# Order of the attention steps' ScalarE copies, output scaling and output-product blocks in a two-block transformer kernel

## The reference

```python
s = jnp.einsum('bnqhgd,bnshd->bnhgqs', qb, kcat, preferred_element_type=jnp.float32)
...
s = jnp.where(valid[None, :, None, None], s - alibi, -jnp.inf)
...
m = jnp.maximum(jnp.max(s, axis=-1, keepdims=True), sink)
p = jnp.exp(s - m)
p = p / (jnp.sum(p, axis=-1, keepdims=True) + jnp.exp(sink - m))
o = jnp.einsum('bnhgqs,bnshd->bnqhgd', p.astype(v.dtype), vcat)
return o.reshape(B, T, N_Q_HEADS * D)
```

## Time and profile before

| | us |
|---|---|
| median of 3 runs | 2187.11 (2186.94 to 2187.57) |
| the profiled execution, own time | 2188.36 |
| its span in the profile | 2186.6 |
| PE busy in the span | 2043.5 |
| DVE busy | 1189.9 |
| ACT busy | 788.7 |
| mean granted TensorE clock, share of full speed | 0.972 |
| attention steps 0 to 35, from and to | 943.5 to 1056.75 |

### The profile page before, as it was taken

How to read it: one execution, slowest core, us unless ns; L and a number is a source line. 1 busy time by engine, 2 the same in 40 slices (tenths; PEclk the granted TensorE clock), 3 DMA queues, 4 the chain that set the end, 5 groups by cost and what they waited for, 6 DMA issues and landing times. The chain is left out here.

```text
span 2186.6 us, 34776 instructions
## 1 busy us (share of the span) xinstructions
PE 2043.5 (93%) x14184; PEld 1598.2 (73%) x14184; DVE 1189.9 (54%) x1773; ACT 788.7 (36%) x1361; POOL 143.9 (7%) x116
## 2 busy tenths in 40 slices
PE   7999999989999999978999999999988859999996
PEld 1577899867787787755788888878843538888884
DVE  5489665565444434655484565755335364565423
ACT  5776333334232212545431212234213234444311
POOL 0000222200101101000010101100000000000000
PEclk9999999989999999999999999999999879999998
DMA  5321000222332232310345354435300112323321
GB/s 178 109 87 39 2 4 4 81 89 87 97 98 94 96 97 81 105 39 21 107 154 191 133 185 144 157 116 190 98 21 0 57 59 89 104 93 99 135 87 39
DMA packets 60393, 200.33 MB, mean 92 GB/s; under 512 B 7904, under 2 KB 10848, under 8 KB 59232
## 3 DMA queue, kind: packets, MB, share of 16 engines
q1 hardware_dynamic: 59808, 193.91, 26.7%
q10 hardware_dynamic: 448, 4.46, 0.5%
HBM read 191.66 MB, written 6.42 MB: 91 GB/s over the span
## 5 line engine op out<-in xcount | busy, mean ns | idle before, releaser
L1129 DVE TENSOR_TENSOR wlo<-raw,whi 128x1024 fp32r<-128x1024 f32 x270 | 327.7, 1223 | 622.0 <-ACT whi L656 620.5
L656 ACT ACTIVATE whi<-raw 128x1024 fp32r<-128x1024 f32 x270 | 282.7, 1057 | 750.0 <-PE bank L1792 732.7
L1790 PE MATMUL bank<-inh,whi 128*128 128x512 f32 x1200 | 473.2, 394 | 26.5 <-DVEq L1725 16.1
L1791 PE MATMUL bank<-inl,whi 128*128 128x512 f32 x1200 | 469.9, 392 | 0.0
L1792 PE MATMUL bank<-inh,wlo 128*128 128x512 f32 x1200 | 469.6, 391 | 0.0
L1790 PEld LDWEIGHTS bank<-inh,whi 128*128 128x128 f32 x1200 | 227.0, 189 | 85.5 <-DVEq L1725 16.9
L1792 PEld LDWEIGHTS bank<-inh,wlo 128*128 128x128 f32 x1200 | 226.9, 189 | 47.7
L1791 PEld LDWEIGHTS bank<-inl,whi 128*128 128x128 f32 x1200 | 227.1, 189 | 47.2 <-issue 0.7
L1790 PE MATMUL bank<-hidh,whi 128*128 128x512 f32 x576 | 231.0, 401 | 5.8 <-DVE HR L1458 4.4
L1791 PE MATMUL bank<-hidl,whi 128*128 128x512 f32 x576 | 227.3, 395 | 0.0
L1792 PE MATMUL bank<-hidh,wlo 128*128 128x512 f32 x576 | 227.2, 395 | 0.0
(11 more groups left out here) (355 smaller groups left out, 2849.3 us busy)
## 6 DMA issues: line engine op xcount, KB each, us to landing
raw<-in_mlp_w SPq DMA_DIRECT2D x128, 512.0 KB, 3.6
ADW<-in_w_ada SPq DMA_DIRECT2D x32, 768.0 KB, 5.0
raw<-in_w_up SPq DMA_DIRECT2D x44, 512.0 KB, 3.5
raw<-in_w_in SPq DMA_DIRECT2D x28, 512.0 KB, 3.6
raw<-in_a_w_rkv SPq DMA_DIRECT2D x24, 512.0 KB, 3.4
raw<-in_w_down SPq DMA_DIRECT2D x22, 512.0 KB, 3.5
raw<-in_a_wo SPq DMA_DIRECT2D x8, 512.0 KB, 8.3
raw<-in_b_wq SPq DMA_DIRECT2D x8, 512.0 KB, 3.3
```

The lines of the kernel that those rows point to most:

```text
L656: act.activation(whi[u % SLOTS][:, :], raw[u % SLOTS][:, :], ACT.Copy).then_inc(w_hi, 1)
L1129: dve.tensor_tensor(lo[:, :], r[:, :], h[:, :].bitcast(F32), ALU.subtract).then_inc(w_lo, 1)
L1790: pe.matmul(o, w[:, wc], xh, start=start, stop=False)
L1791: pe.matmul(o, w[:, wc], xl_, start=False, stop=False)
```

## The change

It has four parts, all in the attention loop. ScalarE's step makes the copy PTR first, then the copy OR, then the exponentials. VectorE's scaling of pair p moves from step 2p+6 to step 2p+5, and the high and low parts of it from step 2p+7 to step 2p+6, so that its loop is one step shorter. TensorE's output-product blocks, two per step, move from steps 10, 11, 14, 15, ... to steps 9, 11, 13, 15, ... up to 35. No instruction is added or removed, and no buffer changes.

```diff
             for i in range(NT + 4):
+                if 2 <= i < NT + 2:
+                    k = i - 2
+                    act.wait_ge(pa.sem, pa.at(("tr", k)))
+                    if k >= 3:
+                        act.wait_ge(pa.sem, pa.at(("pv", k - 3)))
+                    act.activation(PTR[k % 3][:], PB[6][:], ACT.Copy).then_inc(aat.sem, aat.step(("ptr", k)))
+                if i >= 5 and i % 2 == 1:
+                    p = (i - 5) // 2
+                    act.wait_ge(pa.sem, pa.at(("bc", p)))
+                    if p >= 2:
+                        act.wait_ge(da.sem, da.at(("to", p - 2)))
+                    act.activation(OR[p % 2][:], PB[7][:, 0:256], ACT.Copy).then_inc(aat.sem, aat.step(("o", p)))
                 if i < NT:
...
-                if i >= 5 and i % 2 == 1:
...
-                if 2 <= i < NT + 2:
...
-            for i in range(NT + 6):
+            for i in range(NT + 5):
...
-                if i % 2 == 0 and i >= 6:
-                    p = (i - 6) // 2
+                if i % 2 == 1 and i >= 5:
+                    p = (i - 5) // 2
                     dve.wait_ge(aat.sem, aat.at(("o", p)))
...
-                if i % 2 == 1 and i >= 7:
-                    p = (i - 7) // 2
+                if i % 2 == 0 and i >= 6:
+                    p = (i - 6) // 2
...
-                if i >= 10 and (i - 10) % 4 < 2:
-                    kb = (i - 10) // 4
+                if i >= 9 and i % 2 == 1:
+                    kb, q = (i - 9) // 4, (i - 9) // 2 % 2
                     pe.wait_ge(w_lo, UBO + kb // 2 + 1)
                     pe.wait_ge(da.sem, da.at(("ol", 2 * kb + 1)))
-                    for m in range(2 * ((i - 10) % 4), 2 * ((i - 10) % 4) + 2):
+                    for m in range(2 * q, 2 * q + 2):
```

## The result

| | before | after |
|---|---|---|
| median, us | 2187.03 (2184.14 to 2187.57) | 2167.11 (2164.93 to 2168.63) |
| the profiled execution, own time | 2188.36 | 2164.93 |
| its span | 2186.6 | 2163.1 |
| PE busy in the span | 2043.5 | 2039.7 |
| attention, from the scores of step 0 to the rest of the output product, behind step 35 | 943.51 to 1056.75 = 113.24 | 941.02 to 1032.33 = 91.31 |

The changed kernel is faster: 0.9906 of the time before (95% interval 0.9894 to 0.9918), four runs beside four; the two medians alone give 0.9909. The medians differ by 19.9 us; 20.4 were forecast.

A forecast was written before the change was run, and what follows sets the result against it. TensorE, busy 93% of the span, bounds the kernel, with latency gaps in the attention. Start 6.8, four periods 10.3, last period 3.3 and end 0 sum to 20.4 us: 2187.11 - 20.4 = 2166.7, range 2160.5 to 2174.

The forecast's parts named there:

- The gaps are latency between engines, not load.: Attention, four steps: TensorE works 10.60 of 13.04 us, while DVE has only 6.33 and ACT 6.92 us of work.
- The wait labelled "ACT S" is a wait for TO.: Value product's listed 5.2 us wait: really for VectorE's TO, never exponentials; 1.03 us idle in one period.
- The period, 10.46: Four attention steps, 12 to 27: each period takes 10.46 us instead of 13.04, gaining 2.58, or 10.3 over four.
- PTR, exponentials, low part: hidden.: Attention steps: PTR over 1 us spare, exponentials end by S + 3.3 and due S + 5.9, low part S + 2.75 before S + 3.3.
- TO, "the thinnest cover": VectorE: TO ends near 2.7 us after an odd step's scores; the next scores' reading, due at 3.4, has 0.7 spare.
- Weight splits, under 0.1 each.: ScalarE's 1.05 us splits delay the next copy: under 0.1 us in each of three steps, off TensorE's path.
- The start, 6.8.: Steps 0 to 11: 4.7 us of idle gone, 0.5 from the first weight copy, 1.6 from the clock; sum 6.8.
- The end, 3.3 and 0.: Last period (13.79 to 10.46 us) gains 3.3; steps 32 to 35 gain 0, since TensorE has no gap there.
- The clock elsewhere.: Rival behind the attention: 9 us lost to short clock falls may halve (2162) or grow by half (2171); vanishing falls 0.08.
- One wait stays: Rival: VectorE late in even steps or PTR still holds transposes, about 1.0 us per period, 5 in all: 2171.7; chance 0.12.
- Nothing arrives: Rival: the later stage waits for weights and hands the gain back, 2187; chance 0.06 shared with both waits staying.
- Half speed in the dense stretch: Rival, steps 12 to 31: gapless small matmuls get half speed, periods 19.2 us, total 2213; chance 0.04.

The follow-up runs named there:

- extra_copy: Changed kernel with one more 128x512 copy of bank 6 on ScalarE ahead of PTR in 32 steps, into an unused tile; median 2168.83 us, ratio 0.9916.
- undo_dve: Changed kernel with VectorE's old places for TO (even steps) and the low parts (odd steps); median 2195.01 us, ratio 1.0036 to the kernel before.
- only_dve: Kernel before with VectorE's part of the change alone; median 2177.48 us, ratio 0.9960.
- or_last: Changed kernel with ScalarE's copy OR behind the exponentials, PTR still first; median 2168.24 us, ratio 0.9922 to the kernel before.
- undo_act: Changed kernel with ScalarE's old order (exponentials, OR, PTR); median 2167.75 us, ratio 0.9916 to the kernel before.
- V: VectorE's part of the change: TO in odd steps, low parts in even ones; alone on the kernel before, median 2177.48 us, ratio 0.9960.
- only_pe: Kernel before with TensorE's new places of the output-product blocks alone; median 2194.34 us, ratio 1.0034.
- only_act: Kernel before with ScalarE's new order alone; median 2181.76 us of ten runs, ratio 0.9977.
- recip_later: Changed kernel with VectorE's 3.35 us reciprocal of query scales moved from step 1 to step 2; median 2166.86 us, ratio 0.9914 to the kernel before.
- start_both: Changed kernel with VectorE's reciprocal moved to step 2 and two weight splits a step or two later; median 2165.35 us, ratio 0.9899 to the kernel before.
- sums_early: Changed kernel with TensorE's second set of query sums in step 0 instead of step 1; median 2165.13 us, ratio 0.9906 to the kernel before.
- S: ScalarE's part of the change: copies ahead of exponentials; alone on the kernel before, median 2181.76 us, ratio 0.9977.
- T: TensorE's part of the change: output-product blocks in every odd step; alone on the kernel before, median 2194.34 us, ratio 1.0034.

## Why the prediction was right

The forecast was 2166.7 within 2160.5 to 2174.0; the median is 2167.11. It was right in its cause as well, as the parts show, with terms that were off by up to a fifth. That the medians come within 0.5 of the forecast is partly luck: the attention in the trace gained 1.5 more than the sum.

- **"The gaps are latency between engines, not load."** Shown by the result: with no instruction fewer, TensorE idles 0.00 of 10.38 us where it idled 2.44 of 13.04. That ScalarE's load does not bound the changed kernel either is what extra_copy adds: 15.3 us more of its work cost 2.3. VectorE's load was not raised in any run.
- **The wait labelled "ACT S" is a wait for TO.** Shown: with TO back in the even step (undo_dve) the value product waits 1.11 behind it, with it in the odd step (only_dve, and after) there is no such wait, whatever ScalarE's order is.
- **The period, 10.46.** It came out at 10.38 in every period. An odd step takes 2.61 (981.40 to 984.01) instead of 2.62, the even step 2.68 (978.72 to 981.40) instead of 2.66. The 0.08 lies in the first block's even step, which has 10.38 - 2 x 2.61 - 2.68 = 2.48 instead of 2.56: scores to transposes is 0.65 there (984.01 to 984.66), not the 0.75 read in the earlier trace rows.
- **PTR, exponentials, low part: hidden.** No wait for them is left in steps 8 to 35. TO and the exponentials start where the forecast had them: TO 2.23 behind the scores (983.63 after 981.40), exponentials 1.8 and 2.1 behind.
- **TO, "the thinnest cover", 0.7 spare.** Measured 0.73. or_last shows that the other side of the cover, TO ahead of the value product (1.20), is the one that an instruction put ahead of TO uses up first, and that the 0.7 is exceeded without harm in steps without a split.
- **Weight splits, under 0.1 each.** In the changed kernel they cost nothing that 10.38 shows. They are where three of the weakened versions lost most of a period's time: 0.36 in extra_copy, 0.4 to 0.5 more than in periods without a split in undo_act and or_last.
- **The start, 6.8.** Mis-sized by 1.0: 7.8. The idle time of steps 4 to 11 fell from 6.34 to 1.01 (11.28 - 10.27, and 10.39 - 10.39), by 5.3 where 4.7 was forecast. The 0.4 kept for the first product block and 0.1 of each of the two waits of 0.6 were not there: those waits measured 0.51 each. Busy time fell by 1.94 (10.31 + 12.29 before, 10.27 + 10.39 after), where 1.6 was taken for the clock. Not all of it need be the clock: in the four periods the busy time fell too, by 0.9 at a clock of 1.00. The second fall lasts from 964.9 to 968.3 in the kernel before, and 3.4 us at half the clock are 1.7 by an estimate.
- **The end, 3.3 and 0.** Measured 3.5 together.
- **The clock elsewhere.** The term was set at 0 with a range; in this pair of traces it was a gain of 2.5 ahead of the attention and a loss of 0.9 behind it. What the medians of 19.9 and the trace's 21.9 differ by has this size, but what it was in the runs without a trace can't be seen.
- **The rivals.** One wait stays: none did in the periods. Nothing arrives: the idle time behind is the same 1.3 to 1.4 us. Half speed in the dense stretch: did not come, the clock was 1.00 from 963.24 to 1032.33.

**The second fall of the clock.** In the kernel before, TensorE waits at three places between 961 and 965 and then runs at the 1.2 GHz level from 964.81 on (timeline of the kernel before; the value product is in the earlier trace rows):

```profile
961.77 0.70 PE L2198 MATMUL bank<-KD,QF 64*128 64x256 f32 x4 [0.51 <-DVE small L1550]
963.33 0.63 PE L2212 MATMUL bank<-sqs,S 128*128 128x128 f32 x4 [0.86 <-ACT PTR L986]
```

The idle times are 0.51, 0.86 and, in the earlier trace rows, 0.85. In the changed kernel only two waits of 0.51 are left in steps 4 to 8, and the clock stays at 2.4 GHz from 956 on. The combinations agree: the fall stands in all four without V, and in none of the four with it. only_dve keeps the waits of 0.50 and 0.86 in these steps, has no idle time before the value product, and its granted clock from 940 to 975 is that of the changed kernel, 0.90:

```profile
940.00:975.00 35.00, 25.49 (x210) 16.24 (x208) 25.17 (x79) 23.02 (x68) 0.00 (x0) 0.90 0.09 31
```

The kernel before has 0.85 there. The rule of the Trainium skill, "TensorE: Matmul & The Clock Gate", section "A second HAM failure mode: psum-queue depth-cycling", that small idles between groups of matmuls make the clock swing, agrees with this stretch: with most of the idle time gone the fall went, as forecast. It is not enough by itself: the periods from step 12 on in the kernel before idle 2.44 of 13.04 us at a clock of 1.00, and those of undo_dve and only_pe have still more idle time at 1.00. Nor does the length of a wait decide. In step 8 two kernels wait the same for TO; only_act runs the value product behind it at the 1.2 GHz level (1.55),

```profile
973.53 1.55 PE L2233 MATMUL bank<-PTR,VK 128*64 128x128 f32 x12 [2.29 <-DVE TO L1573]
```

and undo_dve at 2.4 GHz (0.88):

```profile
969.49 0.88 PE L2233 MATMUL bank<-PTR,VK 128*64 128x128 f32 x12 [2.28 <-DVE TO L1573]
```

Why the fall comes in steps 6 and 7 in all four kernels without V, once more in steps 8 to 10 in one of them, and in none from step 12 on is open; no kernel was run that adds the idle time there alone. That V removed the fall by removing the wait for TO is therefore argued from eight traces of one execution each, and not shown.

**What stays open.** only_act's granted clock was 0.81 from 940 to 985, against 0.89 in the kernel before; whether its other nine executions had the third fall can't be seen. And in the three start variants a longer stretch at 1.2 GHz takes what earlier readings give: it lasts 10.2 us in each (947.5 to 957.7 in recip_later) and 6.8 in the changed kernel (948.3 to 955.2). In recip_later and start_both it stands behind the same idle time as in the changed kernel (2.42 at the first transposes), in sums_early behind 0.89, 1.09 and 0.78. Why it lasts longer there isn't shown. Last, what S and T each add as the third part rests on single traces.

## What to carry to other kernels

Where streams meet at counting semaphores, look at what stands between the awaited instruction and the one before it that is already free to run: moving short copies that another engine waits for ahead of long work that is due two steps later cost nothing and shortened the attention by 8.5 us once the scaling on VectorE had moved, but by only 4.3 where the product blocks had moved too. Move producers before consumers: the output product put one step earlier shortened it by 3.5 us with its low part moved (S and V there) and lengthened it by 7.7 without. A part of such a change measured alone can have the wrong sign, so read the period in the trace, and try the parts in pairs before one is dropped.

## What was not expected of the hardware

- The same code, ahead of any change, reached the attention between 939.44 and 944.24 us in 14 traces; the granted clock from 450 to 500 us was 0.86 in one and 0.93 in another. A difference of a few microseconds between two single executions says nothing of an edit in this kernel.
- Small edits of the start moved the 1.2 GHz stretch: 3.5 us of full clock lost between 940 and 975 became 5.25 in each of three edits that were meant to shorten it.
- Idle gaps of TensorE of 0.5 to 1.0 us had a fall of the clock behind them at 964.8 and none from step 12 on (1.00 in the earlier trace rows), in the same execution. A wait of 2.3 us in step 8 had a fall with it in only_act and none in undo_dve.
